# The compression network of a sparse attention layer moved among its projections, and the first attention units in another order

## The reference

```python
def compress(kv, pe, w1, b1, w2):          # once for keys, once for values
    ch = kv.reshape(B, S // 16, 16, Hk, d)
    blocks = jnp.concatenate([ch[:, :-1], ch[:, 1:]], axis=2) + pe   # 15 blocks of 32 tokens
    hid = jax.nn.gelu(flat(blocks) @ w1 + b1)                        # 2048 -> 256
    return hid @ w2                                                  # 256 -> 64

s_c = einsum(q, k_cmp) * scale; p_c = masked_softmax(s_c, ...)       # 16 heads x 15 blocks
o_c = einsum(p_c, v_cmp)
# selected branch: top 16 of only 4 blocks of 64 tokens, so all of them: causal attention
# window branch: 512 tokens back of 256, so causal attention as well
o = g0 * o_c + g1 * o_s + g2 * o_w
```

## Time and profile before

| | us |
|---|---|
| median of 3 runs (lowest, highest) | 673.42 (672.68, 677.87) |
| profiled execution | 673.4 |
| its span | 671.6 |
| PE busy | 641.3 (95%) |
| DVE busy | 511.6 (76%) |
| ACT busy | 415.9 (62%) |

### The profile page before, as it was taken

The page is one execution under the profiler, slowest core; times in us unless marked ns, Lnnn a source line. Parts: engine busy times, 40 slices in busy tenths (PEclk is TensorE's granted clock), DMA queues, the critical chain, the costliest instruction groups (busy, mean ns, idle before and its releaser), DMA issues.

```text
span 671.6 us, 11001 instructions
## 1 busy us (share of the span) xinstructions
PE 641.3 (95%) x3662; PEld 537.4 (80%) x3662; DVE 511.6 (76%) x990; ACT 415.9 (62%) x856; POOL 20.8 (3%) x69
## 2 busy tenths in 40 slices
PE   8999989989999999999998999979899999999994
PEld 7988766678888888888887788757788888888893
DVE  4587578965888888888877556796788888888886
ACT  6554367836766666666657445673966666666655
POOL 2100000000000000000002000051000000000000
PEclk9999989999999999999999999999999999999998
DMA  7675020037255555555542545305355555555521
GB/s 274 236 272 205 15 120 2 2 125 251 98 193 191 196 200 196 200 196 198 197 142 75 187 178 188 126 2 196 150 189 189 190 194 187 197 201 196 202 73 64
DMA packets 21442, 109.02 MB, mean 162 GB/s; under 512 B 2592, under 2 KB 2976, under 8 KB 12448
## 3 DMA queue, kind: packets, MB, share of 16 engines
q1 hardware_dynamic: 21120, 108.36, 45.0%
q10 hardware_dynamic: 288, 0.22, 0.1%
HBM read 107.52 MB, written 1.05 MB: 162 GB/s over the span
## 4 chain that ended last, share of the span: by engine, by line
PE 78%; DVE 10%; ACT 5%; issue 3%; POOL 2%; DMA 1%; POOLq 0%; SPq 0%; ACTq 0%; DVEq 0%
PE psA L397 12%; PE psA L398 12%; PE psA L399 12%; PE psO L500 10%; PE psT L500 10%; PE psO L505 5%; PE psT L505 5%; DVE win_lo L1338 2%; DMA stage<-in_w_group 1%; ACT arena L1161 1%; DVE stat L1607 1%; PE psT L676 1%; PE psA L659 1%; DVE x L1388 1%; PE psO L691 1%
## 5 line engine op out<-in xcount | busy, mean ns | idle before, releaser
L1440 DVE TENSOR_TENSOR win_lo<-stage,win_hi 128x1024 fp32r<-128x1024 f32 x90 | 109.6, 1219 | 5.6 <-ACT win_hi L1012 5.6
L1457 DVE SCALAR_TENSOR_TENSOR arena<-arena,prm 128x255 f32<-128x255 f32 (+1 forms) x152 | 73.5, 484 | 50.7 <-ACT arena L1038 48.0
L1012 ACT ACTIVATE win_hi<-stage 128x1024 fp32r<-128x1024 f32 x92 | 96.1, 1051 | 10.0 <-PE psA L399 5.6
L500 PE MATMUL psO<-hA,win_hi 128*128 128x512 f32 x304 | 95.5, 395 | 0.0
L500 PE MATMUL psT<-hA,win_hi 128*128 128x512 f32 x304 | 95.1, 394 | 0.0
L1338 DVE TENSOR_TENSOR win_lo<-stage,win_hi 128x1024 fp32r<-128x1024 f32 (+3 forms) x58 | 64.6, 1154 | 24.8 <-ACT win_hi L948 24.5
L1038 ACT ACTIVATE arena<-arena,prm 128x256 f32<-128x256 f32 x76 | 45.7, 602 | 58.4 <-DVE arena L1463 58.1
L948 ACT ACTIVATE win_hi<-stage 128x1024 fp32r<-128x1024 f32 (+3 forms) x56 | 53.5, 1002 | 28.4 <-PE psA L399 19.2
L397 PE MATMUL psA<-wout_hi,act_hi 128*128 128x512 f32 x176 | 69.2, 393 | 0.7 <-DVE act_lo L1506 0.5
L398 PE MATMUL psA<-wout_lo,act_hi 128*128 128x512 f32 x176 | 68.7, 390 | 0.0
L399 PE MATMUL psA<-wout_hi,act_lo 128*128 128x512 f32 x176 | 68.5, 389 | 0.0
(11 more groups left out here) (287 smaller groups left out, 1218.6 us busy)
## 6 DMA issues: line engine op xcount, KB each, us to landing
stage<-in_w_ffn_in SPq DMA_DIRECT2D x44, 1024.0 KB, 5.5
stage_out<-in_w_ffn_out SPq DMA_DIRECT2D x44, 516.0 KB, 3.6
stage<-in_w_kv SPq DMA_DIRECT2D x8, 1024.0 KB, 4.8
stage<-in_w_group SPq DMA_DIRECT2D x5, 1024.0 KB, 5.0
stage<-in_w_nsa_out SPq DMA_DIRECT2D x4, 1024.0 KB, 5.6
stage<-in_w_dq SPq DMA_DIRECT2D x4, 1024.0 KB, 4.8
stage<-in_w_dout SPq DMA_DIRECT2D x4, 1024.0 KB, 4.8
stage<-in_w_phi SPq DMA_DIRECT2D x2, 1024.0 KB, 4.9
```

Source lines behind the costliest of these rows:

```text
L500: mm(o, win_hi[:, slot, cs], hA[:, k, :, :].rearrange("p a q -> p (a q)"), start=k == 0, stop=False)
L1012: act.activation(win_hi[:, slot, h * W // 2:(h + 1) * W // 2], stage[:, slot, h * W // 2:(h + 1) * W // 2], ACT.Copy).then_inc(sem["in_hi" ...
L1440: last = dve.tensor_tensor(win_lo[:, slot, cs], stage[:, slot, cs], win_hi[:, slot, cs].bitcast(F32), sub)
L1457: dve.scalar_tensor_tensor(conv[:, b, g, k:S], src[:, 0:S - k], prm[:, b, 4 * g + 2 - k:4 * g + 3 - k], conv[:, b, g, k:S], ALU.mult, ALU. ...
```

## The change

All four megabytes of the first product come in 16 pieces of 256 KB, two behind each of the half-groups 3 to 10, into `phi_k1`, `stage_out`, `keysT` and `vals` (the last two are not written until later). The whole first product stands on PE between half-groups 9 and 10, the GELU on DVE and ACT behind it, its transposes between half-groups 10 and 11, and the w2 products right behind the key transposes. The compression scores stand behind the scores of units 0 and 1, and their softmax comes ahead of the units 1 to 3 on DVE. Smaller: in the odd half-groups DVE splits before it rotates; DVE's splits of the output projection's first two half-groups stand in units 10, 11, 14 and 15, and PE does four of the sixteen parts of its first chunk among the last units; one addition in `normalise` goes ahead; the last two steps of the FFN are interwoven, with the splits for the next stage behind; half of the copies into `hB` come after the next split.

```diff
@@ SP: loads of the projections @@
                     i = s - 3
                     cs = slice(i % 4 * 512, (i % 4 + 1) * 512)
-                    sp.dma_start((phi_k1, phi_v1)[i // 4][:, cs], a_phi[1 + 2 * (i // 4)][:, cs]).then_inc(sem[("phi_k_in", "phi_v_in")[i // 4]], 16)
-            for i in range(N_PHI):
-                load(N_A + i, stage[:, i % 2, 0:W], a_phi[2 * i], N_A - 2 + i, None)
+                    half = 1 - i // 4
+                    sp.dma_start((phi_k0, phi_k1)[half][:, cs], a_phi[half][:, cs]).then_inc(sem["phi_k_in"], 16)
+                    sp.dma_start((phi_v0, phi_v1)[half][:, cs], a_phi[2 + half][:, cs]).then_inc(sem["phi_v_in"], 16)
@@ PE: among the projections @@
+            def phi_products():
+
+                pe_.wait_ge(sem["blocks_ready"], 4)
+                pe_.wait_ge(sem["phi_k_in"], 128)
+                pe_.wait_ge(sem["phi_v_in"], 128)
+                for m in range(CP):
+                    for v, pieces in enumerate(((phi_k0, phi_k1), (phi_v0, phi_v1))):
+                        last = mm(psO[v * 64:v * 64 + 64, 0, 0:PHI], blocks[:, v, m, :, :].rearrange("p h i -> p (h i)"),
+                                  pieces[m // 8][:, m % 8 * PHI:(m % 8 + 1) * PHI], start=m == 0, stop=m == CP - 1)
+                last.then_inc(sem["phi_used"], 1)
...
                 if g == 4:
+                    phi_products()
                     pe_.wait_ge(sem["proj_act"], 4)
                     pe_.wait_ge(sem["rope_done"], 3)
-                    q_transposes(range(4))
+                    q_transposes(range(2))
+                    pe_.wait_ge(sem["hid_z"], 1)
+                    q_transposes(range(2, 4))
@@ PE: the first units @@
             pe_.wait_ge(sem["kcmp_ready"], 2)
+            nsa_scores(0)
+            nsa_scores(1)
             cmp_scores()
-            nsa_scores(4)
-            nsa_transpose(2)
+            nsa_transpose(0)
+            nsa_scores(2)
+            nsa_transpose(1)
+            nsa_scores(3)
             pe_.wait_ge(sem["cmp_masked"], 1)
             nsa_pv(0, 0)
+            nsa_transpose(2)
+            nsa_scores(4)
+            cmp_T()
+            nsa_transpose(3)
             nsa_scores(5)
@@ PE: the last units @@
                 nsa_pv(u // 2 - 1, u % 2)
+                if u >= len(UNITS) - 3:
+
+                    i = u - (len(UNITS) - 3)
+                    pe_.wait_ge(sem["negmax"], len(UNITS) - 1 + i // 2)
+                    pe_.wait_ge(sem["probs"], 4 * (len(UNITS) - 1 + i // 2))
+                    out_part(C_WO, hB_hi, hB_lo, 0, 2 * TT, 0, i // 2, (i % 2,))
@@ ACT: end of the FFN (last_steps) @@
+                    for g in range(2):
+                        if g == 1:
+                            act.wait_ge(sem["in_used"], j + (first + 1))
+                        act.activation(conv[:, 0, g, :], (psT, psO)[g][:, 0, 0:S], ACT.Identity,
...
+                    act.activation(silu[:, 0, :], conv[:, 0, 0, :], ACT.Silu).then_inc(sem["silu"], 1)
+                    if layer == 0:
+                        split_in(NJ, 0, 0)
@@ DVE: normalise @@
                 split_first(1)
+                add_y(n, 1, 0, "in_used", chunks)
                 first_mean(n, 0)
-                add_y(n, 1, 0, "in_used", chunks)
@@ DVE: the last units @@
-                if u >= NU - 2:
-                    split(C_WO, (u - (NU - 2),))
+                if u in (10, 11, 14, 15):
+                    split(C_WO + u // 14, (u % 2,))
```

More of the change, by code:

```diff
@@ L306, in _ @@
                 sp.dma_start(x[:, t, 0:D // 2], a_x[0, t]).then_inc(sem[f"x{t}_in"], 16)
[L308 to L314, removed]
             def load_main(s, src, width):
[L317 to L320, removed]
+                if s >= 2:
+                    sp.wait_ge(sem["in_lo"], s - 1)
+                sp.dma_start(stage[:, s % 2, 0:width], src).then_inc(stage_full[s % 2], 16)
             for s in range(N_A):
@@ L604, in _, with hid_T, last_transposes @@
             warm_up(6)
+            def phi_products():
[7 more added lines that the diff above has]
+                last.then_inc(sem["phi_used"], 1)
+            def hid_T():
+                pe_.wait_ge(sem["hid_ready"], 1)
+                pe_.wait_ge(sem["proj_act"], 5)
+                pe_.wait_ge(sem["proj_dve"], 5)
+                for c in range(2):
+                    last = pe_.transpose(psA[:, 0, 0:256].rearrange("p (v c x) -> p c v x", v=2, c=2)[:, c], hid[:, c * P:(c + 1) * P], ident[:, :])
+                last.then_inc(sem["hidT_bank"], 1)
+            def last_transposes():
+                q_transposes(range(4, 8))
+                hid_T()
             for g, (_, width) in enumerate(GROUPS):
@@ L610, in _ @@
                 project(2 * g, hA_hi, hA_lo, [psA[:, 2 * (g % 2) + t, 0:width] for t in range(TT)], width, 4,
[L611 removed]
+                        0 if g == 0 else None, last_transposes if g == 5 else None, x_rest if g == 0 else None)
                 if g == 1:
@@ L1086, in ffn @@
                         step(2 * i + (2 + b), b)
-                step(NJ - 2, 0, layer == 0, False, halves=False)
-                last_step()
+                last_steps()
             act.dma_start(cols[:, 0:O_PE], a_cols[:, 0:O_PE]).then_inc(sem["gains_in"], 16)
@@ L1277, in _ @@
                     split(C_KV + c + 2)
+                if c == 0:
+                    h_hi(hB_hi, O_AG + KT, 2, 2 * KT, range(KT // 2, KT))
             ND = DH // 2 * TT
@@ L1560, in _ @@
                     split(c + 2)
+                if c % 2 and kind == "q":
+                    rope(tokA[:, :, h0:h0 + nh, :], tokB[:, :, h0:h0 + nh, :], nh)
+                if c % 2 and kind == "k":
+                    rope(k_tok, k_tok, 8)
                 if c == 3:
@@ L1644, in copy_pT @@
                 dve.tensor_copy(pT[:, (u // 2) % 2, 0:2 * nb, 2 * m2 + 1, :], psT[:, 1, 0:2 * nb * P].rearrange("p (i q) -> p i q", q=P)).then_inc(sem["pT_dve"], 1)
+            dve.wait_ge(sem["zero"], 2)
+            dve.wait_ge(sem["kcmp_bank"], 1)
+            for e in range(2):
+                dve.tensor_copy(kcT[e * 64:e * 64 + 64, e, :, :].rearrange("p g c -> p (g c)"), psA[e * 64:e * 64 + 64, 1, 0:64]).then_inc(sem["kcmp_ready"], 1)
             maxima(0, 0, "")
@@ L1721, in _ @@
             split(C_KV + 1)
-            h_lo(hB_lo, hB_hi, O_AG + KT)
+            h_lo(hB_lo, hB_hi, O_AG + KT, range(KT // 2))
             ND = DH // 2 * TT
@@ L1769, in _ @@
                     split(C_KV + c + 2)
+                if c == 0:
+                    h_lo(hB_lo, hB_hi, O_AG + KT, range(KT // 2, KT))
             def out_heads(u):
```

212 lines of the change are left out of this document (108 added, 104 removed).

## The result

The changed kernel takes 680.74 us in the median of six runs (678.94 to 683.79), beside 674.02 for the kernel before on the same chip: ratio 1.0094, 95% interval 1.0068 to 1.0120. That is +6.7 us, within 1%, where I had forecast 678.2 and +4.8. Its profiled execution took 680.32 us, and the span is 6.9 us longer than before's. A profile shows one execution: over the six the mean granted clock of the whole span was 0.975 to 0.986, the profiled one's being at the top, so stretches at the lower clock may be longer in the others.

The account below looks back on a forecast made before the run. PE was taken as busy nearly all the span, with DVE pacing the first units. On 673.4 us, 10.4 - 3.4 - 0.6 - 0.6 - 1.0 = +4.8 gave 678.2 us; own range 675 to 681.

Parts of the forecast that it names:

- 1, the blocks: Projections: half-group 10 lands at 54.0, its blocks are ready at 59.9, so PE waits 2.0 us (0.4 to 2.9).
- rival (c): Projections: half-groups 8 and 9 land late enough that PE waits there as well; 680.2 us; chance 0.13.
- 2, up to the first scores: Products +7.2 us, transposes +0.4, wait for kcmp_ready +0.8; with the blocks' 2.0, first scores 10.4 us later.
- 3, the first units: First maximum to the fifth unit's scaling: DVE sets the pace, 21.8 us against 25.25, so -3.4 us.
- Rival (b): First units: clock stays at 1.2 GHz behind the short products until the loop, doubling 5.2 us; 683.4 us; chance 0.12.
- a sign of being wrong: First units: the prediction called itself wrong if the clock stays low past 100 us.
- 4, the late units: Units 10 to 15: output-projection matmuls fill PE's waits, DVE's splits lengthen the chain; -0.6 us (-2.0 to +1.0).
- 5, the small edits: Both normalisations -0.6 us (0.3 each); end of layer 0's FFN -1.0 (-0.5 to -1.2); layer 1 0.

Follow-up runs that it names:

- rotation_first: The changed kernel with DVE rotating before it splits in half-groups 3, 5, 7 and 9, as before: 684.59 us, ratio to the kernel before 1.0155.
- move_only: The changed kernel with all the small reorderings taken back, leaving the compression network's move and the first units' new order: 686.96 us, ratio to the kernel before 1.0184.
- early_scores: The changed kernel with the scores of units 0 and 1 ahead of PE's wait for kcmp_ready: 677.44 us, ratio to the kernel before 1.0053.
- warm_units: The changed kernel with unused matmuls in PE's waits and 8 among the compression scores, and cmp_masked awaited sooner: 677.84 us, ratio to the kernel before 1.0054.
- small_only: The kernel before with only the small reorderings, the compression network staying where it was: 671.34 us, ratio to the kernel before 0.9957.
- ends_only: The kernel before with only the edits to normalisations, FFN last steps and second hidden operand's halves: 672.46 us, ratio to the kernel before 0.9978.
- warm_wait: The changed kernel with 18 unused matmuls of 256 columns in PE's wait for kcmp_ready: 679.03 us, ratio to the kernel before 1.0077.
- small_warm: The kernel before with only the small reorderings, plus 8 matmuls of 256 columns among the compression scores: 671.40 us, ratio to the kernel before 0.9960.

## Why the prediction was right, and where its terms were not

The time (678.2 forecast, 680.7 measured) lies in the forecast's own range of 675 to 681, near its upper end, and the mechanism is the one forecast: work that lay under waits now stands in front of them. That the number came out is partly luck, as the steps show:

**1, the blocks.** PE waited 0.71 us for 2.0. The landing I had put at 54.0 was at the better end, 52.3. rotation_first shows why: with DVE's old order it is 54.24. I had the late landing about right for that order, and costed the edit that takes it away at 0; move_only is rival (c), which the new order of DVE keeps out. By the rate per engine in the Trainium skill ("DMA: Bandwidth & Descriptors", Specifications) no backlog would form. The changed kernel agrees in the landing (ACT's half-group 10 at 52.34), rotation_first doesn't; and neither reached the 464 GB/s estimated from it: from 40 to 50 us the changed kernel's engines moved 360 GB/s at a busy share of 0.99. At that rate 1536 KB take 4.4 us, between the 3.4 and the 5.9 of the forecast.

**2, up to the first scores.** Products 7.06 for 7.2 and kcmp_ready as costed: key copies to first scores 4.7 us (80.98 to 85.67) against 3.9 before, +0.8. early_scores confirms it as a wait on the path. In all +8.7 for +10.4; 1.3 of the difference is step 1, the rest tenths in the other terms. That the 7.2 are uncovered was right for the sum, but not that they could simply be taken away: I had not looked for the wait that is second to them, hid_z behind DVE's split and rotation.

**3, the first units: the step that failed.** Forecast 21.8 us and -3.4, measured 24.3 and -0.8 (and the first maximum itself is 0.5 us later than the first scores, which ran at half clock). DVE's busy time was right (17.1 for 17.4), its waits were not. I had kept the lower clock as a rival with 0.12 and priced it at 0 in the forecast; three stretches of it came. warm_units puts 1.5 us on it (with the sooner wait for cmp_masked in it); the other 1.0 to 1.1 is the wait for the compression scores (1.78, or 1.87 at full clock, for 1.0) and the round trips. Rival (b) was half right: the level did not last from the compression scores on, but came three times, and past 100 us, where the prediction had put a sign of being wrong. The first and the third fall came behind waits (2.10 ahead of 85.67, 1.80 ahead of 106.24). The second, at about 92.6, came with PE busy since 85.67, at the end of the compression scores. Its evidence against, the stretch at 444 us, was one sample of a thing that varies: the clock dropped around there in nine of the fourteen profiled kernels, the changed one (454.5 to 458) among them. PE's lag behind the kernel before grows there from 6.5 us (454.85 for 448.34) to 7.5 (459.28 for 451.77), and is 6.8 again at the end of that layer's output projection (482.55 for 475.76). The Trainium skill's rule ("TensorE: Matmul & The Clock Gate", HAM oscillation) on pauses between bursts fits warm_units, where filled pauses gave 1.00, though that section's pauses are longer than those filled here; small_only's compression scores, at half clock with PE busy without a pause from 85.33 on, are outside it:

```profile
92.00:98.00 6.00, 6.00 (x32) 5.65 (x32) 2.07 (x3) 0.83 (x4) 0.00 (x0) 0.50 0.00 0
```

**4, the late units.** -0.35 for -0.6. The waits of 1.18 and 0.77 ahead of the transpositions of units 14 and 15 are gone, filled by the pieces. The 0.39 and 0.77 shown above are others: they stand ahead of units 12 and 13, where the timeline of before names none, after DVE's two splits in units 10 and 11. (Three parts of the output projection's first chunk stand among the last units; its fourth comes behind them.)

**5, the small edits.** -0.2 in each normalisation and -1.2 at the FFN's end in the traces, for -0.3 and -1.0; DVE's wait of 1.96 is 0.92. ends_only has 1.5 for all of it.

Along PE the forecast was 10.4 us late at the first scores, then 7.0, 6.4 and 6.1 at unit 6's, the end of the output projection and the FFN, 5.1 at the second layer and 4.8 at the end. Measured were 8.7, 8.2, 7.9, 7.7, 6.5 and 6.9. So two errors partly cancel: 1.7 too much up to the first scores and 2.9 too little in step 3; 0.7 more came in the second layer. With the landing as late as forecast the time would have been about 682 (680.7 + 1.3), outside the forecast's own range.

## What to carry to other kernels

Before moving work out of a place where it covers waits, leave it out in an experiment at that place: here 6.2 us of products less gained 0 us there (0.9994, interval 0.9978 to 1.0010), so, as the program stood, moving them away had next to nothing to win. At the new place the same edit shows which wait comes next. Look at the clock in both, for a lower clock can hide what was gained. Where TensorE is the engine that waits, allow for each new wait of a microsecond or two twice, once as idle time and once as work at half clock behind it (not each wait here had that second price). When one change has a move and small edits, time them apart: the small ones alone made the fastest kernel here (0.9957).

## What the hardware did that I had not expected

- 63 matmuls without use, 55 in waits and 8 among short ones (nearly 7 us of work), kept the granted clock at 1.00 from 84 to 112 us and made the kernel 2.7 us faster than the changed one. Against the 18 alone (warm_wait) it is 1.6 us, with intervals that overlap.
- The clock fell with PE busy 6.00 of 6.00 us, in and behind the compression scores, whose 32 matmuls of 32 columns took 5.41 us in small_only and 3.71 before, though nothing in the code had changed there. In ten of the eleven kernels without the 8 wider matmuls the profile shows the lower clock in these scores or within 1 us behind them (in the kernel before from 93.9, behind them); in early_scores it fell only after the next wait. In the three with the 8 it shows 1.00 there; small_warm is the only one of these that differs by nothing else from its partner.
- Leaving out 6.2 us of PE's work made the changed kernel no faster (1.0117 against 1.0094, intervals overlapping): a wait of 3.65 us opened, and the clock was 0.72 instead of 0.82 from 84 to 112 us.
- The DMA's busy share from 40 to 50 us rose from 0.85 to 0.99, and half-group 10 landed no later. With DVE's splits behind its rotations it landed 1.9 us later, at a share of 0.95.
